# A two-block transformer layer: feed-forward products by Strassen's seven blocks, through memory

## The chip, the core and the metric

One core of a Trainium2 chip runs the whole program. Its engines are TensorE (PE in the profile; its weight loads are PEld), VectorE (DVE), ScalarE (ACT), GpSimd (POOL) and SyncE (SP), which issues every DMA here. The time is device microseconds of one execution; the median of a few is given.

## What is computed

Two blocks run in sequence on 1024 tokens of width 1024 in float32. The first has a pooling mixer and a sliding-window attention; the second has two attentions, gates and then the feed-forward part that the change touches:

```
h2 = rms_norm(x, norm2)                            # 1024 x 1024
x  = x + square(relu(h2 @ w_up)) @ w_down           # 1024 x 4096, 4096 x 1024
return rms_norm(x, final_norm)
```

Each float32 operand is split into a high part in TensorE's float32r form and a low part, the rest, and a product is three: high x high, high x low and low x high, with the stationary weights named first.

## The kernel before

Activations are held transposed: features in the partitions, tokens in the columns, two halves of H = 512 tokens, eight feature tiles `k` each. `Hh` and `Hl` are the high and low parts of the normalised input. The feed-forward's 4096 inner features are 32 tiles, and it runs in four chunks of eight tiles. In a chunk, `ev_up` (line 1238 on) takes each product of `wup` out of its bank: relu on ACT (L1238), times the bank on DVE (L1239), high part on ACT (L1241), low part on DVE (L1242), into `Fh` and `Fl`. Then `down` (L1257) multiplies the chunk by `wdn` and adds each of the eight output tiles to the residual stream `xe`. Each output tile of one half takes 24 matmuls of 128 x 128 by 128 x 512: eight `k` by three terms. The last chunk's second half goes in two column quarters of 256, so that the final norm of one quarter lies beside the products of the next; `final` scales the result on DVE (L1285) and stores it.

Weights come as 512 KB loads into `Wr` (three buffers), are cast to `Wh` on ACT (L308) and to `Wl` on DVE (L310; in two earlier stretches POOL does this, `on_pool`), two buffers each. Products go in turn through the three banks `DB`.

The norm of a half (`rstd`, `to_h`, with `norm_h` for this part) sums squares (L417 to L421), gets the reciprocal root in a bank `PV`, and scales `xe` into `hb` on DVE (L453), splits it on ACT (L456) and DVE (L457). The same helpers serve the first block, where line 385 also splits tiles, one of three on POOL; L814 and L816 add a residual there, L502, L713 and L723 are evictions and sums of the first block, L1213 evicts the output projection.

The order in which each engine issues is made by a planner. Every operation is a step of a stream, with a cost in ns and the steps that it waits for; `merge` places at each turn the step that can begin first, streams with lower urgency winning ties, and `emit` writes a wait for each step named. So each engine works through a fixed list, in order, and an operation that waits holds all behind it on its engine, SP's DMA issues too. The planner's costs are 75 + 1.04 n for DVE and 95 + 0.83 n for ACT; it knows of no conflict between engines.

## Time and profile before

| | us |
|---|---|
| median of three runs (lowest to highest) | 1944.43 (1939.92 to 1946.69) |
| span of the profiled execution | 1943.7 |
| TensorE busy | 1901.7 (98%) |
| weight loads busy | 1596.8 (82%) |
| VectorE busy | 1070.6 (55%) |
| ScalarE busy | 743.9 (38%) |
| GpSimd busy | 165.8 (9%) |

The span is from the first to the last instruction. No time of the profiled execution around the span is listed. Displayed durations of following operations on one engine may overlap; the starts tell what each takes of the engine. Idle time of an engine that is not the bottleneck costs nothing.

### The profile page before, as it was taken

Reading aid. Unit: us, or ns where it says so; the run is one execution under the profiler, and the core shown is the slowest. Engines: PE = TensorE matmul, PEld = TensorE weight load, DVE = VectorE, ACT = ScalarE, POOL = GpSimd, SP = SyncE. Lnnn points to the kernel's source line nnn. Section 1 sums busy time; section 2 is a strip of 40 time slices with the busy share of each in tenths; the row PEclk is TensorE's granted clock in tenths of the full one; section 3 lists DMA queues with packets and bytes.
Section 4 is the critical chain, followed back from the end, with each engine's and each line's share of the span. In section 5 each row is a group of like instructions: output and inputs, shape, how many; then the busy total and the mean of one; then the engine's idle time right before and its main releaser. Section 6 shows DMA issues by size and latency. Waiting matters only on the chain.

```text
span 1943.7 us, 24743 instructions
## 1 busy us (share of the span) xinstructions
PE 1901.7 (98%) x9383; PEld 1596.8 (82%) x9383; DVE 1070.6 (55%) x2165; ACT 743.9 (38%) x1416; POOL 165.8 (9%) x199
## 2 busy tenths in 40 slices
PE   8899999989999999999999999999999999999998
PEld 7778777767888888888888888888888888888887
DVE  7898564775788767666733366642233223223355
ACT  6675123444666555555522233431122012102322
POOL 1200011440333210000000000000000000000000
...
GB/s 209 65 23 76 94 44 87 120 109 145 94 77 60 76 70 49 76 67 69 66 225 97 44 137 112 97 95 58 48 50 45 53 44 55 44 55 44 54 96 111
DMA packets 53430, 157.42 MB, mean 81 GB/s; under 512 B 6784, under 2 KB 14272, under 8 KB 52928
## 3 DMA queue, kind: packets, MB, share of 16 engines
...
## 4 chain that ended last, share of the span: by engine, by line
PE 88%; DVE 9%; issue 2%; ACT 0%; DMA 0%; POOL 0%; SPq 0%; DVEq 0%; ACTq 0%
PE D L330 76%; PE PV L1044 3%; PE T L1029 3%; DVE acc L421 2%; PE S L976 2%; PE S L977 2%; DVE SPs L599 1%; DVE SPs L612 1%; DVE PTa L636 1%; DVE xb L816 0%; DVE C L655 0%; PE PV L434 0%; PE PV L445 0%; DVE Hl L385 0%; PE D L552 0%
## 5 line engine op out<-in xcount | busy, mean ns | idle before, releaser
L330 PE MATMUL D<-Hh,Wh 128*128 128x512 f32 (+1 forms) x1712 | 446.4, 399 | 11.0 <-DVE tg L673 3.0
L330 PE MATMUL D<-Hl,Wh 128*128 128x512 f32 (+1 forms) x1712 | 435.3, 393 | 0.0
L330 PE MATMUL D<-Hh,Wl 128*128 128x512 f32 x1696 | 433.2, 394 | 0.0
L330 PEld LDWEIGHTS D<-Hh,Wh 128*128 128x128 f32 (+1 forms) x1712 | 317.9, 189 | 83.2 <-issue 6.5
L330 PEld LDWEIGHTS D<-Hl,Wh 128*128 128x128 f32 (+1 forms) x1712 | 316.7, 188 | 64.9 <-issue 0.5
L330 PEld LDWEIGHTS D<-Hh,Wl 128*128 128x128 f32 x1696 | 315.9, 189 | 62.3 <-DVE Wl L310 0.3
L308 ACT CAST Wh<-Wr 128x1024 fp32r<-128x1024 f32 x188 | 196.9, 1048 | 438.1 <-PE D L330 436.6
L310 DVE TENSOR_TENSOR Wl<-Wr,Wh 128x1024 fp32r<-128x1024 f32 x164 | 200.7, 1224 | 123.1 <-ACT Wh L308 122.9
L1257 DVE TENSOR_TENSOR xe<-D,xe 128x512 f32<-128x512 f32 (+1 forms) x72 | 45.4, 632 | 215.0 <-PE D L330 214.9
L1239 DVE SCALAR_TENSOR_TENSOR tg<-D,tg 128x512 f32<-128x512 f32 x64 | 44.2, 691 | 181.0 <-ACT tg L1238 181.0
L330 PE MATMUL D<-Fl,Wh 128*128 128x512 f32 (+1 forms) x576 | 129.1, 367 | 0.0
L330 PE MATMUL D<-Fh,Wl 128*128 128x512 f32 (+1 forms) x576 | 128.9, 366 | 0.0
L330 PE MATMUL D<-Fh,Wh 128*128 128x512 f32 (+1 forms) x576 | 128.6, 366 | 0.0
L989 ACT ACTIVATE SP<-SP,sm 128x640 f32<-128x640 f32 (+7 forms) x128 | 94.3, 737 | 69.5 <-DVE sm L981 68.0
L1238 ACT ACTIVATE tg<-D 128x512 f32<-128x512 f32 x64 | 38.3, 598 | 213.3 <-PE D L330 213.3
L330 PEld LDWEIGHTS D<-Fl,Wh 128*128 128x128 f32 x576 | 100.7, 189 | 17.9 <-issue 0.5
L330 PEld LDWEIGHTS D<-Fh,Wh 128*128 128x128 f32 x576 | 100.7, 189 | 17.5
L330 PEld LDWEIGHTS D<-Fh,Wl 128*128 128x128 f32 x576 | 100.7, 189 | 17.4
L1036 DVE TENSOR_TENSOR PTb<-T,PTb 128x512 fp32r<-128x512 f32 (+1 forms) x152 | 90.3, 614 | 34.1 <-ACT PTb L1035 33.5
L1035 ACT CAST PTb<-T 128x512 fp32r<-128x512 f32 (+1 forms) x152 | 76.8, 531 | 66.5 <-PE T L1029 51.4
L440 POOL TENSOR_TENSOR rs_t<-ms_t,sm 128x4 f32<-128x4 f32 (+1 forms) x11 | 10.9, 987 | 1062.0 <-DVE ms_t L439 1062.0
L1044 PEld LDWEIGHTS PV<-PTb,V 128*128 128x128 f32 x608 | 85.4, 190 | 7.5 <-DVE PTb L1036 0.2
...
## 6 DMA issues: line engine op xcount, KB each, us to landing
...
K<-K SPq DMA_DIRECT2D x32, 256.0 KB, 3.3
gate_scratch<-tg SPq DMA_DIRECT2D x22, 256.0 KB, 2.1
...
```

Of the source, the lines that this page charges most:

```text
L308: hi = a_w(act(1024), lambda e: e.copy(dst_hi, Wr[:, r, :]), ld, waits)
L310: lo = sub(2400 if on_pool[0] else dve(1024), lambda e: e.tensor_tensor(dst_lo, Wr[:, r, :], dst_hi.bitcast(F32), ALU.subtract), hi, waits)
L330: m = e.matmul(out_ap, st, mv, start=(i + j == 0), stop=(i + j == n - 1))
L421: s = v_sq(dve(n), lambda e: e.tensor_tensor(part, part, hb[:, i, cs], ALU.add), s, acc_free[half])
L976: e.matmul(o, q, sl["K"][:, hh, 0, k0 * 128 + a0:k0 * 128 + a1], start=True, stop=False)
L989: ex = a_exp(act_exp(nk), lambda e: e.activation(buf, buf, ACT.Exp, bias=nm, scale=-1.0, accum_out=ls), mx)
L1029: m = e.transpose(TB[ti][:, o + i * 128:o + i * 128 + 128], SP[:, r["pi"], c0:c0 + 128], ident)
L1035: hi = a_pt(act(off), lambda e, ph=ph, ti=ti, off=off: e.copy(ph, TB[ti][:, 0:off]), t, xold, x_end)
L1036: lo = v_pt(dve(off), lambda e, ph=ph, pl=pl, ti=ti, off=off: e.tensor_tensor(pl, TB[ti][:, 0:off], ph.bitcast(F32), ALU.subtract), hi, xold)
L1044: m = e.matmul(PV[:, qs[0] * 128:qs[-1] * 128 + 128], sl["V"][:, hh, kb, :], p[:, o:o + 128 * len(qs)], start=(i == 0), stop=(i == n_mm - 1))
L1239: v = v_ev(dve(H), lambda e: e.scalar_tensor_tensor(r, DB[d][:, :], 0.0, r, ALU.max, ALU.mult), a)
L1257: f = v_ev(dve(width), lambda e, d=d, xk=xk, width=width: e.tensor_tensor(xk, DB[d][:, 0:width], xk, ALU.add), t, h_ready[half][7], x_done ...
```

## The change

Both feed-forward products are made by Strassen's scheme in Winograd's form: two by two blocks, seven block products and sums of blocks in place of eight block products. Four of the 32 inner tiles stay as they were, in the same way going up and coming down. The other 28 make 14 groups going up, of two tiles each; a block is one weight tile by four `k` and one token half. Coming down, the 14 pairs of inner tiles are contracted in chunks of 2, 4, 4 and 4, for four pairs of output tiles each.

All of up now comes before all of down. So the squared activations, in the seven combinations that are needed as operands, are stored to `f_scratch`, and the residual stream is stored to `x2_scratch`, as `xe` is scaled in place and then serves as staging; it is reloaded at the end of up. The four plain tiles go through `fs_scratch`.

The combined activations going up (`T1` to `T4`) are made once: two differences on DVE, two on POOL and four splits for each of four `k`. The combined weights are made on POOL for every group (`g_s`, four sums), and each of the seven operands is split by `operand` on ACT and DVE into one of four half-size weight slots. A group's products use three banks of one of two sets in the order 1, 6, 2, 7, 5, 4, 3; products 2, 7, 4 and 3 accumulate onto a bank that holds an earlier product, after that product's eviction has read it (`gate`). Going up, the evictions combine with products kept in `tg` and `vt`, square three results on DVE, and POOL makes four differences (`g_t`) for the store. Coming down, every product is added to `xe` on DVE (product 1 by a copy on ACT and three adds on POOL). Operand slots coming down are refilled by `fill`: a 1 MB load (512 KB in the first chunk), then a high part on ACT and a low part on DVE for each two tiles; a slot is loaded only after the last product that reads it, and there are eight slots for the seven operands of a chunk.

Cut to its core:

```diff
+    x2d = nc.dram_tensor("x2_scratch", (2, 128, 8, H), F32, kind="Internal").ap()
+    fd = nc.dram_tensor("f_scratch", (7, 128, 14, H), F32, kind="Internal").ap()
+    fsd = nc.dram_tensor("fs_scratch", (2, 128, 4, H), F32, kind="Internal").ap()
...
+        def ev4s(n, half, d, t):
+            ev4(n, half, d, t)
+            i = n % 4
+            x2_sp[half, n] = x2_prev[i] = dma(d_x2[i], x2d[half, :, n, :], xe[:, half, n, :], 256,
+                                              v_ev.steps[-1], x2_prev[i])
...
+        def norm_h(half, gcol, order):
             rs = rstd(half)
-            for k in range(8):
-                a, lo = to_h(half, k, xe, gcol, rs, h_users[half])
+            for k in order:
+                xk = xe[:, half, k, :]
+                a = v_norm(dve(H), lambda e, xk=xk, k=k: e.scalar_tensor_tensor(
+                    xk, xk, vc[:, gcol + k:gcol + k + 1], PV[:, :], ALU.mult, ALU.mult), rs, x2_sp[half, k], loaded)
+                hi = a_norm(act(H), lambda e, xk=xk, k=k: e.copy(Hh[:, half, k, :], xk), a, h_users[half])
+                lo = v_nlo(dve(H), lambda e, xk=xk, k=k: e.tensor_tensor(
+                    Hl[:, half, k, :], xk, Hh[:, half, k, :].bitcast(F32), ALU.subtract), hi, h_users[half])
+                h_ready[half][k] = [hi, lo]
+                raw_ready[half, k] = a
...
+        def pool2(n):
+            return 342 + 2.46 * n
...
+            fs_spill[half, f] = dma(d_fs[i], fsd[half, :, f, :], r, 256, v, old)
+            r_ring.free(i, fs_spill[half, f])
...
+        for k in range(4):
+            x = {(t, j): xe[:, t, k + 4 * j, :] for t in range(2) for j in range(2)}
+            split_x = {(t, j): h_ready[t][k + 4 * j] for t in range(2) for j in range(2)}
+            def less(e, out, a, b):
+                return e.tensor_tensor(out, a, b, ALU.subtract)
+            t1 = v_t(dve(H), lambda e, x=x: less(e, x[0, 0], x[1, 0], x[0, 0]), split_x[0, 0], raw_ready[1, k])
+            t3 = v_t(dve(H), lambda e, x=x: less(e, x[1, 0], x[1, 1], x[1, 0]), t1, split_x[1, 0], raw_ready[1, k + 4])
+            t2 = g_t(pool2(H), lambda e, x=x: less(e, x[1, 1], x[1, 1], x[0, 0]), t1, t3, split_x[1, 1])
+            t4 = g_t(pool2(H), lambda e, x=x: less(e, x[0, 1], x[0, 1], x[1, 1]), t2, split_x[0, 1])
+            for name, src, done in (("T1", x[0, 0], t1), ("T3", x[1, 0], t3), ("T2", x[1, 1], t2), ("T4", x[0, 1], t4)):
+                sh, sl = slots[name]
+                hi = a_t(act(H), lambda e, sh=sh, src=src, k=k: e.copy(sh[:, k, :], src), done, branch_end)
+                lo = v_t(dve(H), lambda e, sh=sh, sl=sl, src=src, k=k: e.tensor_tensor(
+                    sl[:, k, :], src, sh[:, k, :].bitcast(F32), ALU.subtract), hi)
+                slot_ready[name][k] = [hi, lo]
+                sums_end += [t4, hi, lo]
...
+        def operand(src, kn, *ready):
+            i, old = wq.take()
+            wh, wl = wslot(Wh, i, kn), wslot(Wl, i, kn)
+            hi = a_w(act(128 * kn), lambda e: e.copy(wh, src), ready, old)
+            lo = v_w(dve(128 * kn), lambda e: e.tensor_tensor(wl, src, wh.bitcast(F32), ALU.subtract), hi, old)
+            return i, hi, lo
...
+        product_order = ((1, 0, True), (6, 1, True), (2, 0, False), (7, 1, False), (5, 2, True), (4, 1, False), (3, 2, False))
+        group_n = [0]
+        def seven(jobs, cut, kn, mine, evac):
+            (r0, l0), (r1, l1) = jobs
+            A11, A12 = cut(r0)
+            A21, A22 = cut(r1)
+            sx = [Sx[:, i, 0:128 * kn].rearrange("p (j f) -> p j f", j=kn) for i in range(4)]
+            s1 = g_s(pool2(128 * kn), lambda e: e.tensor_tensor(sx[0], A21, A22, ALU.add), l1, sx_users[0])
+            s2 = g_s(pool2(128 * kn), lambda e: e.tensor_tensor(sx[1], sx[0], A11, ALU.subtract), s1, l0, sx_users[1])
+            s3 = g_s(pool2(128 * kn), lambda e: e.tensor_tensor(sx[2], A11, A21, ALU.subtract), l0, l1, sx_users[2])
+            s4 = g_s(pool2(128 * kn), lambda e: e.tensor_tensor(sx[3], A12, sx[1], ALU.subtract), s2, l0, sx_users[3])
+            source = {1: (A11, l0), 6: (sx[1], s2), 2: (A12, l0), 7: (sx[2], s3), 5: (sx[0], s1), 4: (A22, l1),
+                      3: (sx[3], s4)}
+            set_n = group_n[0] % 2
+            group_n[0] += 1
+            gate = bank_old[set_n]
+            lows = {}
+            for p, bk, first in product_order:
+                src, ready = source[p]
+                w, hi, lo = operand(src, kn, ready)
+                lows[p] = lo
+                name = mine[p]
+                sh, sl = slots[name]
+                bank = banks[set_n][bk]
+                wh, wl = wslot(Wh, w, kn), wslot(Wl, w, kn)
+                terms = [(wh[:, k, :], sh[:, k, :], slot_ready[name][k][0:1] + [hi]) for k in range(kn)]
+                terms += [(wh[:, k, :], sl[:, k, :], slot_ready[name][k]) for k in range(kn)]
+                terms += [(wl[:, k, :], sh[:, k, :], [lo]) for k in range(kn)]
+                t = None
+                for i in range(0, len(terms), 4):
+                    part = terms[i:i + 4]
+                    def emit(e, part=part, i=i, n=len(terms), bank=bank, first=first):
+                        for j, (st, mv, _) in enumerate(part):
+                            m = e.matmul(bank[:, :], st, mv, start=first and i + j == 0, stop=i + j == n - 1,
+                                         skip_group_check=not first)
+                        return m
+                    t = pe(227 * len(part), emit, gate[bk] if i == 0 else None, [s for x in part for s in x[2]])
+                wq.free(w, t)
+                slot_last[name] = [t]
+                gate[bk] = [evac(p, bank, t)]
+            sx_users[:] = [[s2, lows[5]], [s4, lows[6]], [lows[7]], [lows[3]]]
+            raw_ring.free(r0, s2, s3, s4, lows[1], lows[2])
+            raw_ring.free(r1, s1, s3, lows[4])
...
+            def square(i, after):
+                return v_ev(dve(H), lambda e: e.scalar_tensor_tensor(one(i), one(i), 0.0, one(i), ALU.max, ALU.mult), after)
...
+            def evac(p, bank, t):
+                b = bank[:, :]
+                if p == 1:
+                    s["p1"] = a_ev(act(H), lambda e: e.copy(p1b, b), t, held["p1"])
+                    return s["p1"]
+                if p == 6:
+                    s["u2"] = v_ev(dve(H), lambda e: e.tensor_tensor(u2b, b, p1b, ALU.add), t, s["p1"], held["u2"])
+                    return s["u2"]
+                if p == 2:
+                    r = a_ev(act(H), lambda e: e.activation(one(0), b, ACT.Relu), t, old)
+                    f[11] = v_ev(dve(H), lambda e: e.scalar_tensor_tensor(one(0), b, 0.0, one(0), ALU.max, ALU.mult), r)
+                    return f[11]
+                if p == 7:
+                    s["u3"] = v_ev(dve(H), lambda e: e.tensor_tensor(u3b, b, p1b, ALU.add), t, s["p1"], held["u3"])
+                    return s["u3"]
+                if p == 5:
+                    c = v_ev(dve(H), lambda e: e.tensor_tensor(one(2), b, u3b, ALU.add), t, s["u3"], old)
+                    held["u3"] = [c]
+                    f[22] = square(2, c)
+                    return c
+                if p == 4:
+                    c = v_ev(dve(H), lambda e: e.tensor_tensor(one(1), b, p1b, ALU.add), t, s["p1"], old)
+                    held["p1"] = [s["u2"], s["u3"], c]
+                    f[21] = square(1, c)
+                    return c
+                c = v_ev(dve(H), lambda e: e.tensor_tensor(one(7), b, u2b, ALU.add), t, s["u2"], old)
+                held["u2"] = [c]
+                f[12] = square(7, c)
+                return c
...
+            def finish():
+                def diff(o, a, b, *after):
+                    return g_t(pool2(H), lambda e: e.tensor_tensor(one(o), one(a), one(b), ALU.subtract), after)
+                t1 = diff(4, 7, 0, f[12], f[11], old)
+                t2 = diff(5, 2, 4, f[22], t1)
+                t3 = diff(6, 2, 7, f[22], f[12])
+                t4 = diff(3, 1, 5, f[21], t2)
+                sent = []
+                for i, (o0, o1, done) in enumerate(((0, 3, [f[11], f[21], f[22]]), (3, 4, [t4]), (4, 7, [t1, t2, t3]))):
+                    q = (3 * g + i) % 4
+                    sp_prev[q] = dma(d_sp[q], fd[o0:o1, :, g, :].rearrange("o p h -> p o h"), st(o0, o1),
+                                     256 * (o1 - o0), done, sp_prev[q])
+                    sent.append(sp_prev[q])
...
+        fill_order = ["B11", "T2", "B21", "T3", "T1", "T4", "B22", "B12"]
...
+        def fill(src, kn, after):
+            name = fill_order[fill_n[0] % 8]
+            q = fill_n[0] % 4
+            fill_n[0] += 1
+            sh, sl = slots[name]
+            old = slot_last[name]
+            f_prev[q] = ld = dma(d_f[q], sl[:, 0:kn, :].bitcast(F32), src, 256 * kn, after, old, f_prev[q])
+            ready = []
+            for k in range(0, kn, 2):
+                h2, l2 = sh[:, k:k + 2, :], sl[:, k:k + 2, :]
+                hi = a_f(act(1024), lambda e, h2=h2, l2=l2: e.copy(h2, l2.bitcast(F32)), ld, old)
+                lo = v_f(dve(1024), lambda e, h2=h2, l2=l2: e.tensor_tensor(
+                    l2, l2.bitcast(F32), h2.bitcast(F32), ALU.subtract), hi)
+                ready += [[hi, lo], [hi, lo]]
+            slot_ready[name] = ready
+            return name
...
+            def add(half, n, b, t):
+                xk = xe[:, half, n, :]
+                x_add[half, n] = v_ev(dve(H), lambda e: e.tensor_tensor(xk, b, xk, ALU.add), t, x_add[half, n])
+                return x_add[half, n]
+            def add_p1(half, n):
+                xk = xe[:, half, n, :]
+                x_add[half, n] = g_t(pool2(H), lambda e: e.tensor_tensor(xk, xk, p1t, ALU.add), s["p1"], x_add[half, n])
+                return x_add[half, n]
+            def evac(p, bank, t):
+                b = bank[:, :]
+                if p == 1:
+                    s["p1"] = a_ev(act(H), lambda e: e.copy(p1t, b), t, p1_old[par])
+                    p1_old[par] = [add_p1(1, n0 + 1), add_p1(0, n0 + 1)]
+                    return s["p1"]
+                if p == 6:
+                    f = add(1, n0, b, t)
+                    p1_old[par].append(add_p1(1, n0))
+                    return f
+                if p == 2:
+                    return add(0, n0, b, t)
+                if p in (7, 5):
+                    return add(1, n0 + 1, b, t)
+                if p == 4:
+                    return add(0, n0 + 1, b, t)
+                return add(1, n0, b, t)
...
+        for c in range(4):
+            kn = 2 if c == 0 else 4
+            p0 = 0 if c == 0 else 4 * c - 2
+            sent = [s for g in range(p0, p0 + kn) for s in f_spill[g]]
+            mine = {}
+            for p, _, _ in product_order:
+                mine[p] = fill(fd[p - 1, :, p0:p0 + kn, :], kn, sent)
+            for j in range(4):
+                jobs = [raw_job(wdn[c, 2 * j + i, :, 1024 - 256 * kn:1024], 256 * kn) for i in range(2)]
+                seven(jobs, lambda r, kn=kn: down_cut(r, kn), kn, mine, down_evac(2 * j, j % 2))
...
+        std = [fill(fsd[half], 4, [fs_spill[half, f] for f in range(4)]) for half in range(2)]
...
+        def down(n2, half, parts=(every,)):
...
-        for n in range(8):
-            down(3, n, [0])
+        for n2 in range(4):
+            down(n2, 0)
         pv_ring.free(0, final(0))
         quarters = (slice(0, H // 2), slice(H // 2, H))
-        for n in range(8):
-            down(3, n, [1], quarters)
+        for n2 in range(4):
+            down(n2, 1, quarters)
         final(1, quarters[0])
-        final(1, quarters[1], S[0], s_ring.users[0])
+        final(1, quarters[1], S[0], quarter_bank)
```

## Rows read from the trace of the kernel before

**Rows 1.** Page, busy tenths in 40 slices, TensorE and VectorE.
```profile
PE   8899999989999999999999999999999999999998
...
DVE  7898564775788767666733366642233223223355
```

**Rows 2.** Chain that ended last: start, length (us), work.
```profile
1236.72 650.51 PE D L330 x2884
```

**Rows 3.** Stretches: length, PE, PEld, DVE, ACT, POOL busy; clock, DMA share, GB/s.
```profile
980.00:1000.00 20.00, 20.00 (x90) 16.58 (x89) 3.94 (x5) 6.17 (x8) 0.00 (x0) 1.00 1.02 408
1236.70:1887.20 650.50, 650.50 (x2887) 539.33 (x2886) 225.19 (x279) 152.94 (x215) 0.00 (x0) 1.00 0.18 58
```

**Rows 4.** Timeline, end of the output projection; quarters near the end.
```profile
1222.96 1.98 PE L330 MATMUL D<-Hh,Wh 128*128 128x512 f32 x8
1223.16 0.69 DVE L1213 TENSOR_TENSOR xe<-D,xe 128x512 f32<-128x512 f32 x1 [2.48 <-PE D L330]
...
1228.60 0.69 DVE L1213 TENSOR_TENSOR xe<-D,xe 128x512 f32<-128x512 f32 x1 [2.48 <-PE D L330]
...
1902.12 1.03 PEld L330 LDWEIGHTS D<-Fh,Wh 128*128 128x128 f32 x8
...
1903.08 1.03 PEld L330 LDWEIGHTS D<-Fl,Wh 128*128 128x128 f32 x8
```

**Rows 5.** Timeline, independent VectorE operations; a weight load behind one.
```profile
193.61 0.68 DVE L713 TENSOR_TENSOR ub<-D,rsb 128x512 f32<-128x512 f32 x1
194.21 1.22 DVE L310 TENSOR_TENSOR Wl<-Wr,Wh 128x1024 fp32r<-128x1024 f32 x1
195.34 0.70 DVE L723 TENSOR_TENSOR t<-ub 128x527 f32<-128x527 f32 x1
...
1248.97 1.22 DVE L310 TENSOR_TENSOR Wl<-Wr,Wh 128x1024 fp32r<-128x1024 f32 x1
...
1250.24 0.76 PEld L330 LDWEIGHTS D<-Hh,Wl 128*128 128x128 f32 x4 [0.33 <-DVE Wl L310]
```

**Rows 6.** Single lines: min/median/max (ns).
```profile
L385 POOL TENSOR_TENSOR Hl<-C,Hh x6: 1302/1488/2282, 281.1 to 298.1; 128x512 fp32r<-128x512 f32 x6
...
L310 POOL TENSOR_TENSOR Wl<-Wr,Wh x24: 2368/2412/6882, 28.9 to 434.3; 128x1024 fp32r<-128x1024 f32 x24
...
L457 DVE TENSOR_TENSOR Hl<-hb,Hh x4: 679/679/2489, 381.5 to 385.1; 128x512 fp32r<-128x512 f32 x4
```

**Rows 7.** Groups by line: busy us, mean ns.
```profile
L385 POOL TENSOR_TENSOR Hl<-C,Hh 128x512 fp32r<-128x512 f32 x6 | 9.5, 1600 | 134.1 <-ACT Hh L384 134.1
```

**Rows 8.** Timeline where VectorE and GpSimd work together.
```profile
351.21 4.90 DVE L816 TENSOR_TENSOR xb<-xb,y 128x512 f32<-128x512 f32 x8
...
352.09 9.69 POOL L310 TENSOR_TENSOR Wl<-Wr,Wh 128x1024 fp32r<-128x1024 f32 x2 [3.92 <-ACT Wh L308]
...
373.65 2.43 POOL L310 TENSOR_TENSOR Wl<-Wr,Wh 128x1024 fp32r<-128x1024 f32 x1 [4.94 <-ACT Wh L308]
381.06 2.40 POOL L310 TENSOR_TENSOR Wl<-Wr,Wh 128x1024 fp32r<-128x1024 f32 x1 [4.98 <-ACT Wh L308]
...
373.83 2.73 DVE L453 SCALAR_TENSOR_TENSOR hb<-xb,vc,PV 128x512 f32<-128x512 f32 x4 [4.39 <-PE PV L445]
...
381.51 4.29 DVE L457 TENSOR_TENSOR Hl<-hb,Hh 128x512 fp32r<-128x512 f32 x4
```

**Rows 9.** Timeline, second half's norm and the first products going up.
```profile
1237.69 2.72 DVE L453 SCALAR_TENSOR_TENSOR hb<-xe,vc,PV 128x512 f32<-128x512 f32 x4
...
1241.31 0.60 ACT L1238 ACTIVATE tg<-D 128x512 f32<-128x512 f32 x1 [0.25 <-PE D L330]
```

**Rows 10.** Timeline, scaling of the first half of the output.
```profile
1892.35 5.35 DVE L1285 SCALAR_TENSOR_TENSOR xe<-xe,vc,PV 128x512 f32<-128x512 f32 x8
```

**Rows 11.** DMA issues: count, KB each, median us to landing.
```profile
gate_scratch<-tg SPq DMA_DIRECT2D x22, 256.0 KB, 2.1
...
alb<-alibi SPq DMA_DIRECT2D x1, 1024.0 KB, 5.5
```

176 lines of the change are left out of this document (125 added, 51 removed).

## The prediction

> **What bounds the kernel now.** I read the page first: TensorE (PE) is busy to 90% or more in nearly every slice, while the vector engine (DVE) thins out in the last third [rows 1]. The chain of waits says that this stretch is TensorE alone: one unbroken piece of 650.5 us from 1236.7 [rows 2]. The table by stretch gives the room beside it: in those 650 us, at the granted clock 1.00 (2.4 GHz), DVE is busy 35% of the time, the scalar engine (ACT) 24%, GpSimd (POOL) never, and DMA moves 58 GB/s [rows 3]. The prices of a matmul are read from starts: two evictions, 24 matmuls apart, start 5.44 us apart, so 128x512 costs 226.7 ns; eight of 128x256 take 0.96 us, 120 ns each [rows 4]. Fewer matmuls shorten the kernel one for one, as long as the others stay behind them.
>
> **What is removed.** Now the feed-forward has 32 tiles x 2 halves x 24 matmuls going up and as many coming down: 3072 of 128x512 (the last 192 of them as 384 of half width, later 96 as 192; two of these cost 13 ns more than one whole, 1.3 us in all, which I leave out). After: 4 tiles stay plain (192 up, 192 down). The other 28 go as 14 groups of 7 x 12 = 84 in place of 96, and coming down as 14 pairs x 4 column pairs x 21 = 1176 in place of 1344. That is 2736: 336 fewer, x 0.2265 = 76.1 us (one price for all that follows). Base: 1943.7 - 76.1 = 1867.6 us, if every addition is hidden.
>
> **What is added, and where it lies.** Prices: DVE's displayed 0.69 us for 512 columns overlaps the next one's: two independent ones start 0.60 apart, a 1024-column one 1.13 [rows 5]. POOL's 512-column tensor-tensor takes 1.30 us at its fastest and its 1024-column one 2.37 [rows 6]; the slope gives 0.76 for 256. Nothing in the trace shows POOL on a tile with strided pieces; I take 1.30 for it, with 1.60 (the mean of the six, neighbours included) as the upper bound [rows 7].
>
> The two engines exclude each other. At 381 us POOL runs one op of 2.40 us and four DVE subtractions with both inputs in SBUF take 4.29 us, the longest 2.49 against 0.68; the reverse happens at 352, where eight such DVE ops run back to back and the POOL op under them lasts 6.88 us. The DVE ops at 373.8, whose second input is PSUM, ran four in 2.73 us beside a POOL op, untouched [rows 6, 8]. So I keep a second account beside each engine's own: POOL ops plus DVE ops with two SBUF inputs can't exceed the time. The Trainium skill, SBUF — State Buffer, section "SBUF: two separate sides", words this as a lock on a shared port pair that the first comer holds for the whole instruction while the other blocks. With a bandwidth split instead, no account would be full and the time would come near the base; [rows 8] side with the lock.
>
> Per group (PE / DVE all / shared account, us):
> - going up: PE 84 x 0.2265 = 19.0. DVE 7 weight lows, 6 adds or relu products from PSUM, 3 squares: 16 x 0.60 = 9.6. Account: 10 x 0.60 + 8 POOL ops (4 weight sums, 4 differences) x 1.30 = 16.4.
> - coming down, full: PE 19.0. DVE 7 lows + 6 PSUM adds = 7.8. Account: 4.2 + 7 x 1.30 = 13.3.
> - coming down, first chunk (2 of 4 tiles deep, four groups): PE 9.5. DVE 7 x 0.40 (the slope from 1.13 to 0.60 gives 0.34, rounded up) + 3.6 = 6.4. Account 2.8 + 4 x 0.76 + 3 x 1.30 = 9.7: already over.
> - each refilled operand slot: 1 MB read and 2 x 1.13 = 2.3 of DVE, all on the account.
>
> Everything is therefore hidden inside most groups; these are the places where it isn't.
> 1. Before the first group (six DVE and two POOL ops per `k`) the 16 combined operand blocks need 24 DVE and 8 POOL ops. The scaling of the second half begins at 1237.7 and the second plain product ends at 1241.3 [rows 9]; six more and one of the first group's give 1241.3 + 32.6 + 2.7 = 1276.6, when T2 is wanted: 38.9 us; T4 is wanted 10.9 later. DVE 36.6, account 24.8 + 4.8 (norm lows) + 7 x 1.13 + 5.2 (first weight sums) = 42.7, not all of it due at the first of the two. Bounds 0 and 10; I take 4.
> 2. A product accumulates onto a bank that the product before last wrote, so its first matmul waits for that eviction: three on DVE per group, one product of cover (2.72 us). The eviction takes 0.69 and some 0.25 for the two hand-offs (PE to DVE 0.2, DVE to PE 0.05 [rows 4, 5]). With one locked op ahead: 1.30 + 0.60 + 0.94 = 2.84, late by 0.1; with two, 4.7, late by 2.0. I take 0.2 in each of the 42 gates going up and 0.1 in the 36 of the full groups down: 12 us. Bounds 0 and 78 x 0.7 = 55.
> 3. Last group up into the first chunk: until the seventh slot is wanted, 19.0 + 8.2 = 27.2 us, against 16.4 + 8.4 + 7 x 1.13 = 32.7 on the account: 5.5.
> 4. The first chunk: 9.7 + 0.6 (prefetch) against 9.5 in three groups, 2.4, and 12 gates with a cover of 1.36 only, 0.4 each: 7.2.
> 5. First chunk into the second: a slot is refilled only when the last group has used it. 9.5 + 16.3 = 25.8 us, need 9.7 + 11.4 + 6 x 2.26 = 34.7: 8.9. The two later chunk changes: 35.3 us, need 13.3 + 11.4 + 13.6 = 38.3: 3.0 each.
> 6. The end: final scaling of the first half is 5.35 us of DVE; now it lies beside quarter products of 2.88 us each, then of 12 x 0.12 = 1.44 with three banks: 5.35 + 0.42 - 2.88 = 2.9, say 3 [rows 10]. The 13 us after the last product stay.
>
> Sum: 4 + 12 + 5.5 + 7.2 + 8.9 + 6 + 3 = 46.6.
>
> Other moves cost nothing: ACT has per group up 7 casts, a copy and a relu, 9 ops of some 0.6 us [rows 9], 5.4 of 19. DMA: 2.75 MB per 19 us going up, about 150 GB/s; at the change of item 5, 7.4 MB in 25.8 us, 300 GB/s, where 20 us at 408 GB/s are on record [rows 3]. A single 1 MB load lands after 5.5 us [rows 11] and four refill queues run at once; if only 260 GB/s came, 4 us there. The second residual stream is stored before its in-place scaling: 256 KB lands in 2.1 us [rows 11], behind the 9 us from the last eviction at 1228.6 [rows 4] to the scaling. SP's queue has five issues per group; each can hold a weight load behind its wait, but raw weights are wanted 10 us later.
>
> **Forecast.** 1867.6 + 46.6 = 1914.2; the runs' median stands 0.7 above the profiled span (1944.4 against 1943.7; the page gives no time around the span), so 1915. Its own range, each place between half and 1.5 times its price: 1891 to 1938.
>
> **Rivals.**
> - *The covers hold.* Planned order keeps evictions ahead of the other DVE work and POOL's ops slip into the gaps, so only DVE's own total counts: item 5 has 6.4 + 6.7 + 13.6 = 26.7 against 25.8, and item 6: 1867.6 + 1 + 3, and 2 for the first place: 1874. For it: DVE at half load, POOL's ops wanted 10 us later. Against: the account of 86% in each group up.
> - *The additions bound the group; slower.* One mechanism: POOL at 1.60 per op and nothing of DVE beside it. Group up 9.6 + 12.8 = 22.4 (+3.4, x14 = 47), full group down 7.8 + 11.2 + 4 of refill = 23.0 (+4.0, x12 = 48), first chunk 6.4 + 8.8 + 0.6 = 15.8 (+6.3, x4 = 25): 1867.6 + 120 + 3 = 1991. It decides from 76 / 28 = 2.7 us lost per group of 19, one product; going up that is POOL at 1.52 per op. For it: the six-op mean of 1.60, and POOL's starving under a DVE chain. Against: the DVE ops from PSUM ran beside POOL. The Trainium skill, Perfetto Trace Analysis, section "Optimizing Scalar/DVE Operations", warns that moving work between DVE and GpSimd might not help, since they share a port; by it the POOL sums are worth no more than on DVE.
> - *Refills bound by transfer.* 260 GB/s at all four changes: 6 us more, 1921; not told from the forecast by time, only by who is waited for.
>
> **Numbers.** Forecast, with the refill rival in it, 0.60; covers hold 0.18; additions bound 0.17; between, about no change, 0.05. A difference under 0.3% (5.8 us) can't be told from none here. Faster 0.77, same 0.05, slower 0.18. The range reaches into both sides: 1870 (covers hold) to 1955.
>
> **What would show it.** 432 fewer matmul instructions than 9383 (336, and 96 for halves now whole), 226 ns apart inside a group, clock 1.00. Going up the groups should repeat in 19.0 to 20 us; 22 is the second rival. POOL's sums at 1.3 to 1.6 us, DVE's two-SBUF ops stretched to 2 us at times, its PSUM ones not. TensorE's waits should name DVE's evictions and low parts, most at the first chunk and at its end; if they name DMA, transfers were dearer than I think. I am wrong if TensorE's waits are spread evenly at 2 us or more a group, or if strided POOL ops cost over 1.6.

## The result, and the profile after

The changed kernel takes 1931.76 us (median of four runs, 1928.44 to 1934.6) against 1943.52 for the kernel before (four runs beside it): ratio 0.9938, 95% interval 0.9918 to 0.9958. It is 11.8 us faster; 1915 was forecast. The profiled execution has a span of 1928.4 us, 15.3 less than before. Of that, 5.0 us lie ahead of the change: the same matmuls of the norm's sums start at 1232.0 in the trace of before and at 1227.0 here, as the first part varies between executions. From that point the change gave 10.3 us. 76.1 us of matmuls are gone, so about 66 us came back as waits, where 46.6 were forecast.

The page, in the slices of [rows 1]:

```profile
PE   8899999989999999999999999989999977989897
...
DVE  7898564785788767665733366686666688677656
...
POOL 1200001440333210000000000157565666655520
PEclk9999999999999999999999999989999989999998
```

From up on, VectorE rose from 2 to 4 tenths to 5 to 8, GpSimd from nothing to 5 to 7. TensorE has dents at slice 27, the start of up, at 33 and 34, from up into down and into the second chunk, and at 36 and 38, the two later chunk changes.

The chain of waits answers to [rows 2]. Its columns are start, length and work:

```profile
1317.11 19.04 PE D L1371 x84
1336.15 10.88 PE S L1371 x48
...
1545.62 11.32 DMA Hl<-f_scratch
1556.97 1.05 ACT Hh L1494
1558.04 1.83 DVE Hl L1495
1559.87 0.61 DVE xe L1510
1560.53 5.13 PE D L1371 x12
...
1707.04 11.62 PE D L1371 x40
1718.66 10.88 PE S L1371 x48
1737.70 19.04 PE D L1371 x84
```

Going up, a group takes 19.04 us, which is 84 x 226.6 ns, with no wait; all groups after the first do. The unbroken 650 us of before are now cut at few, large places. The 12 matmuls from 1560.53 take 5.13 us, 0.427 each: after a stand TensorE runs at the lower of its two levels (1.2 GHz) for a while. The stretches show it (columns as in [rows 3]):

```profile
1238.50:1279.83 41.33, 35.49 (x151) 28.21 (x150) 40.02 (x47) 20.94 (x34) 21.86 (x12) 0.94 0.31 108
1279.83:1545.30 265.47, 265.47 (x1160) 219.55 (x1161) 173.95 (x226) 77.10 (x128) 160.38 (x108) 0.99 0.49 163
1545.30:1602.00 56.70, 45.34 (x182) 34.63 (x180) 47.58 (x62) 21.23 (x40) 41.24 (x32) 0.91 0.57 210
1602.00:1632.35 30.35, 19.64 (x73) 14.33 (x74) 28.12 (x26) 14.35 (x19) 16.16 (x8) 0.89 0.41 162
1690.80:1709.00 18.20, 12.19 (x49) 9.38 (x48) 18.20 (x18) 8.47 (x11) 11.24 (x4) 0.89 0.31 111
```

Where TensorE is never idle (the second row) VectorE is busy 66% and GpSimd 60% of the time. Where it loses time, VectorE is full: 40.0 of 41.3, 28.1 of 30.4, 18.2 of 18.2.

I sum what TensorE lost: between the starts of successive weight loads, what exceeds 226.5 ns by over 60 ns. "Cold" matmuls (some 0.20 us over) are in it. The numbers in front are the items of the forecast.

| place | lost, us | forecast |
|---|---|---|
| 1, start of up (1.3 before, 9.4 in the first group) | 10.7 | 4 |
| 2, bank gates, groups up 2 to 14, and full groups down | 0 | 12 |
| 3, first group down (one stand of 8.5, to 1560.53) | 10.6 | 5.5 |
| 4, the other three groups of the first chunk | 4.6 | 7.2 |
| 5, first to second chunk | 15.6 | 8.9 |
| 5, second to third, third to fourth (1.4 of each in the last group before) | 10.4, 10.0 | 3.0, 3.0 |
| last group to the plain tiles | 1.6 | 0 |
| 6, end (one stand of 3.4, to 1900) | 4.0 | 3 |
| sum | 67.5 | 46.6 |

Before, the same sum up to the last product is 0.8. What both kernels lose behind the last product, waiting for the final norm (3.5 before, 4.5 here), isn't in the table. So 67.5 - 0.8 = 66.7 stands beside the 66 from the spans.

A timeline of the stand at the second to third chunk:

```profile
1694.19 9.98 POOL L1515 TENSOR_TENSOR xe<-xe,tg 128x512 f32<-128x512 f32 x3 [8.22 <-ACT tg L1521]
...
1697.39 1.21 DVE L1495 TENSOR_TENSOR T<-T 128x1024 fp32r<-128x1024 f32 x1
...
1698.53 0.68 DVE L1510 TENSOR_TENSOR xe<-D,xe 128x512 f32<-128x512 f32 x1
1699.13 3.92 DVE L1495 TENSOR_TENSOR T<-T 128x1024 fp32r<-128x1024 f32 x2
...
1702.97 0.68 DVE L1510 TENSOR_TENSOR xe<-D,xe 128x512 f32<-128x512 f32 x1
1703.57 2.81 DVE L1495 TENSOR_TENSOR T<-T 128x1024 fp32r<-128x1024 f32 x2
1706.31 1.28 DVE L1324 TENSOR_TENSOR Wl<-Sx,Wh 128x512 fp32r<-128x512 f32 x2
1707.04 1.35 PEld L1371 LDWEIGHTS D<-T,Wl 128*128 128x128 f32 x4 [6.10 <-DVE Wl L1324]
```

TensorE waits for a weight low part. VectorE is never idle here; it makes low parts of refilled slots (L1495) ahead of it. The pair at 1699.13, beside GpSimd's additions, takes 3.92 us where two take 2.34 undisturbed (at 1690.52). Over the 14 low parts made between 1680.3 and 1707.0, most took 1.21 us, and six were stretched to 1.7 to 2.3. The pair at 1703.57 belongs to the slot of the following chunk's first product, which TensorE wants some 70 us later.

Single lines, minimum, median and maximum in ns, against [rows 6]:

```profile
L1495 DVE TENSOR_TENSOR T<-T x28: 1205/1452/2318, 1536.9 to 1854.2; 128x1024 fp32r<-128x1024 f32 x28
L1515 POOL TENSOR_TENSOR xe<-xe,tg x48: 1254/1738/5594, 1553.9 to 1849.0; 128x512 f32<-128x512 f32 x48
L1510 DVE TENSOR_TENSOR xe<-D,xe x48: 676/691/692, 1548.5 to 1842.6; 128x512 f32<-128x512 f32 x48
L1441 POOL TENSOR_TENSOR xe<-xe x52: 1287/1514/1760, 1300.2 to 1533.0; 128x512 f32<-128x512 f32 x52
```

VectorE's low parts of refills are stretched to as much as 2.32 us, GpSimd's additions to 5.59, VectorE's operations with a PSUM input never.

### The profile page after: what moved, and what is told of

Read it like the earlier page. It is cut to its first block, busy times and chain, and to the rows that moved or that the text cites. A ratio compares the mean times of both kernels' runs of the same rounds, so it can differ in the third digit from the quotient of the medians.

```text
span 1928.4 us, 25186 instructions
## 1 busy us (share of the span) xinstructions
PE 1840.4 (95%) x8951; PEld 1533.6 (80%) x8951; DVE 1308.9 (68%) x2442; ACT 816.6 (42%) x1555; POOL 530.1 (27%) x431
## 4 chain that ended last, share of the span: by engine, by line
PE 80%; DVE 14%; issue 4%; DMA 1%; ACT 1%; POOL 0%; SPq 0%; DVEq 0%; ACTq 0%; POOLq 0%
PE D L335 44%; PE D L1371 12%; PE S L1371 9%; PE PV L1049 4%; PE T L1371 3%; PE T L1034 3%; PE S L981 2%; PE S L982 2%; DVE acc L426 2%; DVE T L1495 1%; DVE Hl L1495 1%; DVE xe L1510 1%; DVE Wl L1324 1%; DVE SPs L604 1%; DVE SPs L617 1%
## 5 line engine op out<-in xcount | busy, mean ns | idle before, releaser
L335 PE MATMUL D<-Hh,Wh 128*128 128x512 f32 (+1 forms) x1264 | 334.7, 401 | 10.7 <-DVE tg L678 3.1
L335 PE MATMUL D<-Hl,Wh 128*128 128x512 f32 (+1 forms) x1264 | 324.0, 393 | 0.0
L335 PE MATMUL D<-Hh,Wl 128*128 128x512 f32 x1248 | 320.4, 394 | 0.5 <-DVE Wl L315 0.5
L335 PEld LDWEIGHTS D<-Hh,Wh 128*128 128x128 f32 (+1 forms) x1264 | 232.9, 189 | 65.3 <-issue 6.6
L335 PEld LDWEIGHTS D<-Hl,Wh 128*128 128x128 f32 (+1 forms) x1264 | 232.2, 187 | 47.5 <-issue 0.5
L335 PEld LDWEIGHTS D<-Hh,Wl 128*128 128x128 f32 x1248 | 229.9, 188 | 44.9 <-DVE Wl L315 0.9
L1324 DVE TENSOR_TENSOR Wl<-Sx,Wh 128x512 fp32r<-128x512 f32 (+1 forms) x120 | 105.9, 886 | 49.6 <-ACT Wh L1323 48.7
L1371 PE MATMUL D<-T,Wh 128*128 128x512 f32 x416 | 108.9, 403 | 17.0 <-DVE xe L1510 8.7
L1515 POOL TENSOR_TENSOR xe<-xe,tg 128x512 f32<-128x512 f32 x48 | 85.7, 1811 | 103.6 <-ACT tg L1521 99.0
L1371 PEld LDWEIGHTS D<-T,Wh 128*128 128x128 f32 x416 | 80.3, 195 | 37.1 <-DVE xe L1510 10.2
```

Of the source, the lines that this page charges most:

```text
L335: m = e.matmul(out_ap, st, mv, start=(i + j == 0), stop=(i + j == n - 1))
L1324: lo = v_w(dve(128 * kn), lambda e: e.tensor_tensor(wl, src, wh.bitcast(F32), ALU.subtract), hi, old)
L1371: m = e.matmul(bank[:, :], st, mv, start=first and i + j == 0, stop=i + j == n - 1, skip_group_check=not first)
L1515: x_add[half, n] = g_t(pool2(H), lambda e: e.tensor_tensor(xk, xk, p1t, ALU.add), s["p1"], x_add[half, n])
```

## The experiments

The theory at the outset was the account of the forecast: the exclusion of VectorE and GpSimd fills the chunk changes. Its rivals were the order in which VectorE works and late transfers. "A place" below is one of the table above, with the same sum. Several runs leave out work; their own expectations say which. Runs without an interval are single. Four to ten executions of one kernel span 2.6 to 11 us here, and in the profiles of this study the same matmul of the first plain product is reached anywhere from 1243.4 to 1251.2. So these runs are read place by place. The first group up, which most edits leave alone, loses between 8.2 and 9.7 us in those runs, so a difference under 1.5 us at a place says nothing.

**Order by priority.** The casts and low parts of the refills get a lower priority in the planner than those of the weights.

```diff
-        a_f = Stream(P, "scalar", "act_fill", 4)
-        v_f = Stream(P, "vector", "dve_fill", 4)
+        a_f = Stream(P, "scalar", "act_fill", 6)
+        v_f = Stream(P, "vector", "dve_fill", 6)
```

> The refill's casts and low parts get a lower rank in the planner than the weights' (urgency 6 in place of 4), so where several steps could begin at the same moment the weights and evictions go first. If the order of the queues makes the loss at the chunk changes (TensorE stood 6 us at 1701 and at 1787 for a weight low part that was queued behind four refill low parts), the two later changes lose 3 us each in place of 10, and the time falls by 10 to 18 us, to about 1917. If VectorE and GpSimd simply have too much work there, the wait moves from the weight low parts to the refill low parts and the time stays within 4 us of 1931.8. If late transfers are the cause, nothing changes either, and the wait of 8.5 us at 1552 stays.

Measured 1928.45 (1923.59 to 1931.49), ratio 0.9917, interval 0.9892 to 0.9942. First group down 7.9, second chunk 13.5, later changes 9.7 and 9.6: 0.4 to 2.7 us less per place. The planner only breaks ties by priority; a step that can begin first still goes first.

**Without the refills' low parts.**

```diff
-                    l2, l2.bitcast(F32), h2.bitcast(F32), ALU.subtract), hi)
+                    l2[:, :, 0:8], l2[:, :, 0:8].bitcast(F32), h2[:, :, 0:8].bitcast(F32), ALU.subtract), hi)
```

> The refill's low parts are computed for 8 of 512 columns only (part of the computation is left out): 52 VectorE operations of 1.13 us become short ones. If VectorE's load at the chunk changes is the cause, the changes into the second, third and last chunk lose under 3 us each (35 us less in all, about 1898). If late transfers are the cause, the 8.5 us at the end of the up part and most of the change into the second chunk stay: 1915 to 1920.

1899.06. The later changes lose 0.4 and 0.5 (were 10.4 and 10.0), the second chunk 3.3 (was 15.6). So without the low parts on VectorE nearly all of item 5 goes. The first group down keeps 9.4 (7.2 in one stand).

**Without the refills' bytes.** Loads of 16 columns.

```diff
-            f_prev[q] = ld = dma(d_f[q], sl[:, 0:kn, :].bitcast(F32), src, 256 * kn, after, old, f_prev[q])
+            lw = H if name == "B12" else 16
+            f_prev[q] = ld = dma(d_f[q], sl[:, 0:kn, 0:lw].bitcast(F32), src[:, :, 0:lw], 256 * kn, after, old, f_prev[q])
```

> The refill loads bring 16 of 512 columns (all of them for one of the eight slots), so the operands coming down are wrong data; casts and low parts run in full. If late transfers are the cause, the wait of 8.5 us at the change from up to down goes, and the change into the second chunk loses 5 us less: 1912 to 1918. If VectorE's load is the cause, the three chunk changes coming down stay as they are (16, 10 and 10 us) and only the first one shrinks: 1920 to 1928.

1933.67; second chunk 15.0, later changes 10.7 and 10.0. Transfers are not what TensorE waits for at the changes. In the first group down 9.4 is left, and the stand is now VectorE's alone (its timeline):

```profile
1557.97 2.28 DVE L1496 TENSOR_TENSOR T<-T 128x1024 fp32r<-128x1024 f32 x1
1560.18 2.28 DVE L1496 TENSOR_TENSOR Hl<-Hl,Hh 128x1024 fp32r<-128x1024 f32 x1
...
1562.38 1.47 DVE L1511 TENSOR_TENSOR xe<-D,xe 128x512 f32<-128x512 f32 x2
1563.11 1.35 PEld L1371 LDWEIGHTS D<-T,Wh 128*128 128x128 f32 x4 [7.27 <-DVE xe L1511]
```

**GpSimd's work coming down made small.** Weight sums and additions of 8 columns.

```diff
+            fc = slice(0, 8) if down_now[0] else slice(0, 128)
...
-                x_add[half, n] = g_t(pool2(H), lambda e: e.tensor_tensor(xk, xk, p1t, ALU.add), s["p1"], x_add[half, n])
+                x_add[half, n] = g_t(pool2(H), lambda e: e.tensor_tensor(xk[:, 0:8], xk[:, 0:8], p1t[:, 0:8], ALU.add), s["p1"], x_add[half, n])
```

> GpSimd's weight sums and additions coming down are done for 8 columns of each tile only (part of the computation is left out): 7 operations a group of 1.3 to 2.3 us become short, VectorE keeps all its own. If the two engines' exclusion makes the loss, VectorE alone has 22 to 26 us of work in windows of 26 to 35 and the three chunk changes coming down lose 10 us or less together (36 now): about 1905. If the queue order makes it, a weight low part still stands behind four refill low parts of 1.13 us and 4 us stay at each: about 1918. If transfers make it, the time stays above 1925.

1911.04. Second chunk 7.9, later changes 4.7 and 4.8: half is gone. The first group down has 9.7.

**Combinations.** The first two leave-outs together, then all three.

> The last two cuts together: refill loads of 16 columns (all for one slot) and refill low parts of 8 columns (part of the computation is left out). Each alone left the wait at the change from up to down at 7.2 us (8.5 with neither). If a late transfer and VectorE's backlog lie side by side there, each hiding the other, the wait falls under 2 us, and the time lies 8 to 10 us under that of the run without low parts (1899): about 1890. If the wait has a third cause (the weight loads, the additions on GpSimd), it stays near 7 and the time at 1898.

> Refill loads, refill low parts and GpSimd's work coming down all cut short (part of the computation is left out). If these three are all that the change from up to down and the first chunk lose by, the first group down loses under 2 us (6.7 with GpSimd's work in, 9.5 to 10.6 otherwise) and the others nothing: about 1885. What is then left is the start, the last change and the end: 16 us. If the short groups' bank hand-overs (1.36 us of cover) cost by themselves, 0.5 to 1 us a group stays in all four groups of the first chunk.

1895.29 and 1890.46. The first group down falls to 6.7 and then to 4.0 (one stand of 2.4). Each of the three alone left it at 9.4 to 9.7, the lower priority of the refills at 7.9: there a late load and VectorE's backlog lie side by side, and either one holds TensorE.

**The start.** The two block sums per `k` that GpSimd makes go to VectorE (`g_t` becomes `v_t`, twice).

> The eight sums that make T2 and T4 before the first group run on VectorE in place of GpSimd: 8 x 0.60 in place of 8 x 1.30 to 3.4 us. If the two engines' exclusion makes the loss before the first products (9.4 us in the first group), it falls by 3 to 6 us (about 1927). If VectorE's own queue is the bound there, it rises by up to 5 us (1933 to 1937).

1933.46. First group up 6.5 (was 9.4), the plain products before it 2.1 (was 1.3): 2 us less at the start, which the whole of one run can't show.

**Going up only.** Up as changed, down as eight block products: four operand slots per chunk, no differences and no additions on GpSimd.

```diff
-                t1 = diff(4, 7, 0, f[12], f[11], old)
-                t2 = diff(5, 2, 4, f[22], t1)
-                t3 = diff(6, 2, 7, f[22], f[12])
-                t4 = diff(3, 1, 5, f[21], t2)
...
-                seven(jobs, lambda r, kn=kn: down_cut(r, kn), kn, mine, down_evac(2 * j, j % 2))
...
+            for half, i, o in ((0, 0, 0), (0, 1, 1), (1, 0, 3), (1, 1, 2)):
+                mine[half, i] = fill(fd[o, :, p0:p0 + kn, :], kn, sent)
```

> Seven products going up only; coming down the 28 tiles are multiplied plainly, from four operand slots a chunk that are refilled while the other four are read (eight slots as before), and GpSimd makes no differences and no additions. TensorE gets 168 matmuls back: 38 us. If the loss lies at the chunk changes coming down (57 us there with the plain last part), it goes and the time is 1931.8 + 38 - 50 = about 1915 to 1922, faster than with both. If storing and reloading by itself is what costs, some 20 us stay at the changes: 1935 or more.

1923.62 (1921.91 to 1925.34), ratio 0.9898, interval 0.9879 to 0.9917. With the next run, which is as fast, it is the fastest kernel of this study that computes everything, though it runs 168 matmuls more than the changed one (38.1 us). Its chain is one piece coming down, and by the sum of the table it loses 19.1 us in all, against 67.5:

```profile
1552.49 328.71 PE D L335 x1464
```

So Strassen coming down gives 38.1 us of matmuls and costs 48 in waits.

> Seven products going up only, and the block sums before the first group on VectorE: the two edits that each gained. The first group loses 2 us less than in the run with the first edit alone: 1920 to 1923, against 1923.6. If the two do not add up, 1924.

1924.29 (1922.71 to 1926.1), ratio 0.99 (0.9887 to 0.9912): with the start's sums on VectorE as well, nothing more.

**A planner that knows the exclusion.** From the feed-forward on, GpSimd's steps may not overlap in the plan with VectorE's low parts (weights, refills, norm) and block sums, and a GpSimd step costs 225 + 2.1 n. VectorE's squares were left free.

```diff
+                    if st.shared:
+                        t = max(t, port)
...
-            return 342 + 2.46 * n
+            return 225 + 2.1 * n
```

> The kernel after with a planner that knows of the exclusion from the feed-forward on: GpSimd's sums and VectorE's weight, refill, norm and block low parts may not overlap in the plan, and a GpSimd sum costs 1.30 us for 512 columns in place of 1.60. Same operations, other order. If the order is to blame for the chunk changes, 10 us or more come back: 1915 to 1922. If the work on the two engines is too much there whatever the order, it stays within 5 us of 1931.8.

1940.67 (1936.02 to 1942.52), ratio 0.9979, interval 0.9967 to 0.999: worse. Later changes 9.3 and 10.8, second chunk 16.8, three groups after the first 6.8 (was 4.6), the start 12.4 (was 10.7). This plan moved the stands and removed none. That it fails because it still has no due times is not shown.

**GpSimd's three additions coming down moved to VectorE.** (`g_t` becomes a stream `v_a` on VectorE.)

> Coming down, the three additions of product 1 per pair of output tiles run on VectorE in place of GpSimd: 3 x 0.60 in place of 3 x 1.3 to 5.6 us. The shared account of a full group falls from 13.3 to 11.2 and of a later chunk change from 38.3 to 34.4 in 35.3 us, that of the first chunk's groups from 9.7 to 7.6 in 9.5; VectorE's own work rises to 9.6 and 31.4. If the exclusion is the bound, the two later changes lose 5 us less each and the first chunk with its change 8 less: 1910 to 1918. If VectorE's own queue is the bound, everything gets worse by about 1.8 us a group there: 1935 to 1945.

1932.19 (1925.18 to 1936.24), ratio 0.9935, interval 0.9918 to 0.9952: as the changed kernel. Second chunk 12.2, later changes 10.4 and 9.8. The stretching goes away and VectorE's own work takes its place (its timeline):

```profile
1701.18 4.62 DVE L1496 TENSOR_TENSOR T<-T 128x1024 fp32r<-128x1024 f32 x4
1705.72 1.28 DVE L1516 TENSOR_TENSOR xe<-xe,tg 128x512 f32<-128x512 f32 x2
1706.93 0.68 DVE L1324 TENSOR_TENSOR Wl<-Wr,Wh 128x512 fp32r<-128x512 f32 x1
```

Four low parts take 4.62 us here, where two pairs took 3.92 and 2.81 above. The other three groups of the first chunk lose 6.8 (was 4.6). The forecast of this run by the exclusion alone, 5 us less at each later change, failed, and I needed another theory.

**The weight sums going up made twice.**

> Going up, GpSimd makes each of the four weight sums twice (the same result): GpSimd's own work rises from 10.4 to 15.6 us of a group's 19.0, the shared account from 16.4 to 21.6. If the account holds, a group takes 21.6 us or a little more in place of 19.04 (2.6 x 14 = 36 us, about 1968). If only GpSimd's own time or a soft slowing counts, the groups stay at 19.04 and the time within 5 us of 1932.

2014.12. A group takes 24.1 us, 5.1 more, for four operations of about 1.35 us. Both theories missed it: GpSimd isn't full, it waits for the next weights. The groups by line:

```profile
L1349 POOL TENSOR_TENSOR Sx<-Wr 128x512 f32<-128x512 f32 x26 | 36.7, 1412 | 88.3 <-DMA Wr<-wup 87.2
```

Load, sums, low parts and release of the raw buffer form a ring: in this trace the last sums end at 1413.6 and the last low part made from a raw tile at 1414.7, the two loads are issued at 1414.8, and the next sums begin at 1419.6. The added time lengthens the group nearly one for one. The plan differs too, as it now puts differences between the sums, so how little the changed kernel had to spare in this ring, where no group waits, isn't shown.

**Does the form of the operation matter?** The trace has the 39 squares going up, one tensor as both inputs, at 681 to 689 ns, never stretched. I took the form to be free of the exclusion and put squares in place of the refills' low parts, then of all low parts coming down.

```diff
-                lo = v_f(dve(1024), lambda e, h2=h2, l2=l2: e.tensor_tensor(
-                    l2, l2.bitcast(F32), h2.bitcast(F32), ALU.subtract), hi)
+                lo = v_f(dve(1024), lambda e, h2=h2, l2=l2: e.scalar_tensor_tensor(
+                    l2, l2.bitcast(F32), 0.0, l2.bitcast(F32), ALU.max, ALU.mult), hi)
```

> Leaves out: coming down, the low part of a refilled operand slot is the square of the loaded tile, computed on VectorE with one SBUF tensor as both inputs, in place of tile minus high part; as many operations of as many columns as in the changed kernel, with the same waits. Going up VectorE's squares (39 of 39 at 681 to 689 ns) were never stretched, but most of them also met no GpSimd operation, so this run also tells whether that form is free of the exclusion. If it is free: the refill's share of the exclusion goes away and VectorE's own work stays. Theory A (at a chunk change VectorE's own in-order queue is the bound, the exclusion only stretches it by a third): the operations fall from a mean of some 1.47 to 1.13 us, 14 of them return about 4.8 us, and the lost time falls from 10 to 5 or 6 us at each of the two later changes and from 20 to 13 to 15 at the first; whole 1931.8 - 16 = 1916. Theory B (the exclusion is the bound, without it the changes would be covered): under 2 us at each later change, 1905. If the form is not free: operations stretched as before, 1930 to 1934, every place within 1 us.

> Leaves out: coming down, the low parts of the refilled slots and of the weight operands are squares of one SBUF tensor in place of differences of two; number, columns and waits unchanged. With this, VectorE has no operation with two different SBUF inputs coming down, so if the form is free of the exclusion nothing on VectorE and GpSimd can hold the other up. Theory A (VectorE's own queue): the evictions and the weight lows still stand behind 12 to 14 operations of 1.13 us, so 4 to 6 us stay lost at each later change and 12 or more at the first with the change before it; whole 1912 to 1917, GpSimd's adds all near 1.25 us. Theory B (exclusion): no more than 2 us at each later change, whole under 1905. If the form is not free: as the changed kernel, 1930 to 1934.

1933.5 and 1928.79, no place changed by more than 2.4 us. The squares are stretched as the differences were (fill_squares, then all_squares_down):

```profile
L1495 DVE SCALAR_TENSOR_TENSOR T<-T x28: 1207/1223/2321, 1538.7 to 1858.1; 128x1024 fp32r<-128x1024 f32 x28
```

```profile
L1327 DVE SCALAR_TENSOR_TENSOR Wl<-Sx x64: 410/694/1767, 1539.3 to 1850.1; 128x512 fp32r<-128x512 f32 x48, 128x256 fp32r<-128x256 f32 x16
```

One tensor read twice counts as two inputs. Going up the squares were short because none of the 39 met a GpSimd operation, as in the changed kernel's timeline of one group, where GpSimd's sums end at 1426.5 and its differences begin at 1433.5:

```profile
1427.26 0.68 DVE L1407 SCALAR_TENSOR_TENSOR xe<-xe 128x512 f32<-128x512 f32 x1
...
1424.80 1.74 POOL L1347 TENSOR_TENSOR Sx<-Wr,Sx 128x512 f32<-128x512 f32 x1
1433.47 6.06 POOL L1441 TENSOR_TENSOR xe<-xe 128x512 f32<-128x512 f32 x4 [6.93 <-DVE xe L1407]
```

In `sums_twice_up`, where GpSimd works longer, more than half of the same squares lie beside a GpSimd operation and take up to 1.80 us:

```profile
L1412 DVE SCALAR_TENSOR_TENSOR xe<-xe x39: 692/807/1802, 1296.5 to 1591.2; 128x512 f32<-128x512 f32 x39
```

**Work that isn't due, put behind work that is.** The whole computation, in another order. In `spare_later` the refill for the next chunk's first product waits for its chunk's second group; `spread3` and `spread4` also hold back the low parts of the last four or three slots until the product three or four before has ended.

```diff
+                late = [group_end[-3]] if c > 1 and p == 1 else []
-                mine[p] = fill(fd[p - 1, :, p0:p0 + kn, :], kn, sent)
+                mine[p] = fill(fd[p - 1, :, p0:p0 + kn, :], kn, sent + late, c > 0 and p in LAZY)
...
+                if name in lazy_lows:
+                    lazy_lows.pop(name)(ends[-LEAD])
```

> Whole computation. Each chunk coming down refills seven slots; the first refill of the next chunk goes to the slot that this chunk leaves free, so it can be loaded at once, and the trace of the changed kernel has its two low parts on VectorE inside the change of chunk (two T at 1703.57, just ahead of the weight low part at 1706.31 that TensorE waits for until 1707.04; two Hl at 1624.08 ahead of the wait that ends at 1627.08), 60 us before TensorE wants them. Here this one load waits for the end of the second group of its chunk, when VectorE has room. Nothing else changes. Queue theory (TensorE's stand at a chunk change is the backlog of VectorE's in-order work there, 14 refill operations of which 2 are not due): 2 x 1.13 to 1.40 us are taken out of the backlog, so the stand shrinks by 2.3 to 2.8 and the cold matmuls by some more: from 10.3 and 9.9 lost at the two later changes to 7 to 8 each, from 15.6 to 12.5 to 13.5 at the first; whole 1931.8 - 7 = 1925. Exclusion theory: the work is the same, only moved out of a window whose account is too full, so it expects the same 2.3 to 2.8. The rival that the bound is the landing of transfers or the order of the last weight operand expects under 1 us at each place, 1930 to 1933.

1930.7 (1928.82 to 1935.29), ratio 0.9931, interval 0.9911 to 0.9951. Later changes 7.5 and 8.5, second chunk 14.2; of the 5.8 us won at the three, 3.1 come back as stands in the third groups, where the moved work now lies.

> Whole computation. As spare_later, and in addition the low parts of the last four refilled slots of a chunk (of its products 7, 5, 4 and 3) are each made only after the end of the product three before in the chunk's first group, so that VectorE doesn't work ahead of evictions and weight low parts on slots that TensorE wants 6 to 11 us later. In the changed kernel all 14 were done at 1706.3, when TensorE had 40 of the group's 84 matmuls still to issue. Order theory (VectorE has the capacity, but does work that isn't due ahead of work that is): the two later changes fall to 2 to 5 us, the first to 8 to 10; whole 1931.8 - 7 - 12 = 1913. Capacity theory (each product of that group needs 2.26 + 0.60 + 0.60 = 3.5 us of VectorE against 2.72 of TensorE, more with the exclusion, so that waiting only moves the work to where there is no room): no gain over spare_later or a loss, three or four stands of 1 to 2 us in place of one of 6; 1925 to 1932.

1931.63 (1930.25 to 1936.51), ratio 0.9938 (0.9923 to 0.9954). Later changes 7.5 each, but in three stands and with 5.8 in the third groups: too late.

> Whole computation. As spread3, but the low parts of the last three slots only (products 5, 4 and 3), each after the end of the product four before. Order theory: between spare_later and spread3 or a little better than either, because VectorE starts on a slot one product earlier: later changes 2 to 6 us each, whole 1912 to 1918. Capacity theory: as spare_later, 1925.

1927.9 (1926.9 to 1929.46), ratio 0.9916, interval 0.9901 to 0.993. Later changes 6.1 and 6.0, second chunk 13.5. Of the 8.3 us won at the two later changes 4.2 come back as stands in third groups. All three intervals overlap with that of the changed kernel, so none is shown to be faster as a whole, and each gained less (0.1 to 3.9 us) than the order theory expected (7 to 20).

**Order and exclusion together.** `spread4` with GpSimd's work small.

> Leaves out: coming down, GpSimd's weight sums and residual additions cover 8 columns of each tile in place of all (their number and waits unchanged), on top of the order of spread4. So neither work done before it is due nor the exclusion is left at the chunk changes; VectorE's own due work is. Mixed theory (of the 10 us at each later change some 5 are the exclusion and the rest is order): the later changes fall from 4.7 to under 1 us each, the first from 13.5 to 4 to 6, the stands of 1.8 and 1.4 us in third and fourth groups vanish; the sum of the losses coming down falls from 46 to 20 to 24 and the whole to about 1904. Capacity theory (VectorE's own 3.5 us a product in a change's group is more than 2.72): the later changes stay at 3 to 5 us as with GpSimd's work made small alone (4.7 and 4.8), whole 1910 to 1912.

1899.54. With the two single edits this makes a square ("all coming down" is without the end):

| | second chunk | later changes | all coming down | whole |
|---|---|---|---|---|
| changed kernel | 15.6 | 10.4, 10.0 | 52.7 | 1931.76 |
| order (`spread4`) | 13.5 | 6.1, 6.0 | 46.3 | 1927.9 |
| GpSimd small | 7.9 | 4.7, 4.8 | 29.4 | 1911.04 |
| both | 4.1 | 0, 0 | 16.2 | 1899.54 |

With both, the chain of this run shows the groups around the later changes (1678.45 to 1697.49 is the third chunk's first) unbroken at 19.04 us:

```profile
1659.41 10.88 PE S L1381 x48
1678.45 19.04 PE D L1381 x84
1697.49 10.88 PE S L1381 x48
...
1754.85 19.04 PE D L1381 x84
1773.89 10.88 PE S L1381 x48
```

## Why the prediction was right and wrong

**Right.** The direction; 432 fewer instructions (8951 against 9383), 226.6 ns from one to the next inside a group; the exclusion in both directions, PSUM inputs untouched; who is waited for (evictions and low parts, DMA but once); the end (4.0 for 3). Groups repeat in 19.04 us, going up and, away from the changes, coming down, so the additions don't bound them, and that rival is out. "The covers hold" is right for item 2, wrong for 1, 3 and 5.

**Item 2, the bank gates: 12 us forecast, 0 found.** I charged every eviction the meeting with a locked operation. In steady groups VectorE is idle a third of the time, and a cover of 2.72 us was enough in all of them. A price per event times 78 events was wrong in kind: the wait shows where VectorE has a backlog and nowhere else. In the full groups at the chunk changes TensorE does stand behind evictions, 5.5 us in all, and these are counted under item 5. Twice 1.4 us of it lie in the last group of a chunk, where an eviction comes after two stretched refill low parts:

```profile
1683.11 3.95 DVE L1495 TENSOR_TENSOR Hl<-Hl,Hh 128x1024 fp32r<-128x1024 f32 x2
...
1686.98 0.68 DVE L1510 TENSOR_TENSOR xe<-T,xe 128x512 f32<-128x512 f32 x1
...
1687.71 1.70 PEld L1371 LDWEIGHTS T<-T,Wh 128*128 128x128 f32 x8 [1.39 <-DVE xe L1510]
```

**Item 5, the chunk changes: 14.9 forecast, 36.0 found. This is the step that failed.** I set all work on the shared account against the length of two groups, "35.3 us, need 38.3", as if work could be spread over the window. It can't be: a slot comes free one product at a time, a load follows, and the backlog then stands in VectorE's one in-order queue ahead of evictions and weight low parts. From 1680.3 to 1707.0 that queue made 14 refill low parts, two of them not due for 70 us. The square splits the 10 us of a later change: with GpSimd's work small 4.7 are left, with the other order 6, with both nothing. So beside a small GpSimd, VectorE has the capacity for its own due work, and at the change itself each of two causes is worth 4 to 6 us: the plan's order, and GpSimd's work that stretches VectorE's. By itself the order is worth only half of that, as 4.2 of its 8.3 us come back in third groups; beside the small GpSimd work these stands are gone too (0.5 left). On moving work out of GpSimd's way, the Trainium skill, Perfetto Trace Analysis, section "Optimizing Scalar/DVE Operations", warns that moving work between these two engines may not help because they share a port; the move of the additions agrees in its outcome (0.9935 against 0.9938); its trace gives another reason, that VectorE's own queue is full at the changes.

**Item 3, up to down: 5.5 forecast, 10.6 found.** I had left out the late load. A load of 1 MB lands after 11.3 us here and after 5.6 to 7.4 at the median, by its tile; in [rows 11] it was 5.5. It lies beside the backlog of VectorE: each leave-out alone takes 1 us off the place, which is within the noise, the lower priority 2.7, all three leave-outs together 6.6.

**Item 1, the start: 4 forecast, 10.7 found.** The account asked for 42.7 us in 38.9, and I took 4 of a bound of 10, as if part of the work could wait; VectorE is busy 40.0 of 41.3 us and makes none of it up. The stands are 4.2 us to 1276.2 and 2.3 to 1279.8, behind the high and low parts of block sums. With GpSimd's eight block sums on VectorE the place loses 8.6.

**Item 4** was priced at 7.2 and cost 4.6. **Not in the sum at all:** the lower clock after each stand. Matmuls take 0.20 us more for 7 to 15 of them after each long stand, about 10 us in all, which are inside the places above.

**The balance.** 67.5 - 46.6 = 20.9 us more were lost than forecast, and item 5 alone is 21.1 over. That the rest came out even is luck: items 1, 3, 6 and the change to the plain tiles cost 14.4 more than their prices, items 2 and 4 cost 14.6 less. The profiled span is 14.2 over the 1914.2 of the sum: 20.9 less the 5.0 by which the first part was shorter in this execution, less 1.7, of which 1.3 are the half-width products that the forecast left out. The median of the four runs lies 16.8 over 1915.

**Open.** What holds the last 2.4 us of the first group down. How much of GpSimd's share is the stretch of VectorE's operations and how much the lateness of its own sums, since making them small shortens both; moving only the additions to VectorE did not separate them. The leave-outs, two rows of the square among them, are single runs. A version with due times in the planner wasn't tried, nor was Strassen coming down with fewer refilled slots.
